# An MLP and an attention moved from a two-block tail into the loop over gathered experts

## What is computed

```python
def peer_ffn(h, w_q, sub_keys, u_tab, v_tab):      # last layer of the first network, per block of 128 rows
    ...                                            # 8 heads; each picks 16 of 16384 experts per row
    act = jax.nn.gelu(jnp.einsum('thkd,td->thk', u_tab[idx], xb)) * wts
    return jnp.einsum('thk,thkd->td', act, v_tab[idx])

def sq_relu_mlp(x, w1, w2):                        # w1 1024 x 4096, w2 4096 x 1024
    return jnp.square(jax.nn.relu(x @ w1)) @ w2

def second_block(x, ...):
    for i in range(DEPTH):                         # DEPTH = 2
        if i % 2 == 0:
            h = mixer_sb_ssm(x, ...)               # stick-breaking attention and a state space scan
        else:
            h = mixer_dsa(x, ...)                  # 16-head attention over keys that an index selects
        x = layer_norm_2(ALPHA * x + h, ln_mix_g[i], ln_mix_b[i])
        x = layer_norm_2(ALPHA * x + sq_relu_mlp(x, mlp_w1[i], mlp_w2[i]), ln_ffn_g[i], ln_ffn_b[i])
    return x
```

## Time and profile before

| | us |
|---|---|
| median of three executions | 3682.71 |
| the profiled execution, device time | 3654.87 |
| its span, first to last instruction | 3653.6 |
| TensorE busy | 2616.1 (72%) |
| VectorE busy | 2061.5 (56%) |
| ScalarE busy | 518.2 (14%) |
| GpSimd busy | 1516.7 (42%) |
| mean granted clock of TensorE, of full speed | 0.821 |
| read from memory | 1152.84 MB |

### The profile page before, as it was taken

How to read it: one execution, slowest core, us unless ns; L and a number is a source line. 1 busy time by engine, 2 the same in 40 slices (tenths; PEclk the granted TensorE clock), 3 DMA queues, 4 the chain that set the end, 5 groups by cost and what they waited for, 6 DMA issues and landing times.

```text
span 3653.6 us, 35023 instructions
## 1 busy us (share of the span) xinstructions
PE 2616.1 (72%) x12888; PEld 1202.7 (33%) x12888; DVE 2061.5 (56%) x5112; ACT 518.2 (14%) x1007; POOL 1516.7 (42%) x1609
## 2 busy tenths in 40 slices
PE   6688777755556865655588585556665889899998
PEld 1233222111112321111154221112312575767765
DVE  0367777656667667866404577666898354231411
ACT  1121011100012111100022110001210122020200
POOL 0035556546666666666500156666566210000000
PEclk8889888788667887767789687776867899999999
DMA  8789999999999999999822599998999786667577
GB/s 308 257 310 363 357 393 379 403 401 389 366 350 364 385 367 354 337 361 366 310 104 81 208 364 391 363 366 333 393 358 347 263 303 223 207 256 253 216 246 263
DMA packets 363672, 1156.36 MB, mean 317 GB/s; under 512 B 33712, under 2 KB 33968, under 8 KB 362476
## 3 DMA queue, kind: packets, MB, share of 16 engines
q0 software_dynamic: 232144, 849.51, 61.4%
q1 hardware_dynamic: 130940, 304.36, 23.2%
q10 hardware_dynamic: 416, 0.23, 0.0%
HBM read 1152.84 MB, written 1.15 MB: 316 GB/s over the span
## 4 chain that ended last, share of the span: by engine, by line
PE 39%; DVE 21%; DMA 20%; POOL 8%; issue 7%; another core or an unknown queue 3%; ACT 2%; SPq 0%; DVEq 0%; ACTq 0%; POOLq 0%
DMA BIG<-in_p_v_dram,IDX 12%; POOL BIG L2363 8%; PE PS L1158 8%; DVE BIG L1959 8%; PE PS L1092 7%; PE PS L1380 6%; PE PS L1362 6%; DMA BIG<-in_p_u_dram,IDX 4%; PE PS L1256 2%; PE PS L1350 2%; DMA WR<-in_w_mod_dram 1%; PE PS L1120 1%; DVE SC L2157 1%; DVE I L1883 1%
## 5 line engine op out<-in xcount | busy, mean ns | idle before, releaser
L1158 PE MATMUL PS<-BIG,DG 64*64 64x512 f32 x6144 | 1057.6, 814 | 674.0 <-DMA BIG<-in_p_v_dram,IDX 500.4
L2363 POOL DMA_INDIRECT BIG<-in_p_u_dram,IDX x768 | 735.1, 957 | 1021.4 <-ACT SCU L1525 242.5
L1959 DVE CUSTOM_DVE_ANT_0 BIG<-BIG,PS 128x1024 f32<-128x1024 f32 x768 | 927.9, 1215 | 312.7 <-DMA BIG<-in_p_u_dram,IDX 272.9
L2363 POOL DMA_INDIRECT BIG<-in_p_v_dram,IDX x768 | 738.6, 962 | 345.7 <-issue 180.4
L1158 PEld LDWEIGHTS PS<-BIG,DG 64*64 64x64 f32 x6144 | 274.4, 168 | 1342.3 <-issue 1220.1
L1092 PE MATMUL PS<-WR,HT 128*128 128x512 f32 x640 | 297.8, 619 | 10.0 <-DMA WR<-in_a_w_in_dram 4.6
L1362 PE MATMUL PS<-HT,WR 128*128 128x128 f32 x2048 | 259.8, 288 | 5.5 <-DVE mv L1807 4.9
L1362 PEld LDWEIGHTS PS<-HT,WR 128*128 128x128 f32 x2048 | 251.0, 203 | 15.5 <-issue 8.9
L1380 PE MATMUL PS<-WR,BIG 128*128 128x512 f32 x512 | 226.2, 597 | 0.0
L1092 PEld LDWEIGHTS PS<-WR,HT 128*128 128x128 f32 x640 | 123.5, 198 | 177.2 <-issue 168.5
L1380 PEld LDWEIGHTS PS<-WR,BIG 128*128 128x128 f32 x512 | 97.1, 192 | 117.4 <-issue 117.1
(11 more groups left out here) (320 smaller groups left out, 2714.0 us busy)
## 6 DMA issues: line engine op xcount, KB each, us to landing
WR<-in_mlp_w_dram SPq DMA_DIRECT2D x128, 1024.0 KB
WR<-in_w_mod_dram SPq DMA_DIRECT2D x48, 1024.0 KB
WR<-in_b_w_in_dram SPq DMA_DIRECT2D x18, 1024.0 KB
WR<-in_a_w_in_dram SPq DMA_DIRECT2D x16, 1024.0 KB
WR<-in_p_w_q_dram SPq DMA_DIRECT2D x16, 1024.0 KB
BIG<-in_dsa_w_dram POOLq DMA_DIRECT2D x16, 1024.0 KB, 7.6
BIG<-in_p_u_dram,IDX POOLq DMA_INDIRECT x768
BIG<-in_p_v_dram,IDX POOLq DMA_INDIRECT x768
```

The lines of the kernel that those rows point to most:

```text
L1158: mm = self.e.matmul(pv[64 * i:64 * i + 64, 2 * r + n, :], dg[p, :], row[p, n * 512:n * 512 + 512], start=h == 0 and j == 0, stop=h == 7 a ...
L1959: self.e.tensor_tensor_reduce(row, row, xp, 1.0, 0.0, ALU.mult, ALU.add, m.ACTV[:, u % 4, j:j + 1]).then_inc(*self.done("dot", l, u, j))
L2363: self.e.indirect_dma_start(row, None, m.A[f"p_{table}"], bass.IndirectOffsetOnAxis(ap=m.IDX[:, u % 4, j:j + 1], axis=0)).then_inc(*m.GR.l ...
```

## The change

The background of block 1's experts is no longer mixer 0 of block 0 alone but a chain (`block_ahead`): mixer 0, stepped with 1 instead of 2 waiting steps, MLP 0 and mixer 1 of block 0. This MLP is cut into parts (`mlp_parts`): part s makes slab s of the up product, squares it, and adds the down product of slab s - 1 into `X` at once, so that `F` (which lies where the gathers go) is not needed. Two yields of a part go to one step of the loop (`"more"`). In the loop a part's PSUM comes from the 2-bank ring (`place` 0), in the tail from the banks of `UP` and `DOWN` (`place` 1). What is left of the chain when the loop ends runs before the barrier.

The tail has then: mixer 0 of block 1 with the first five parts of block 0's MLP 1; block 1's MLP 0 alone; mixer 1 of block 1 with the parts left; block 1's MLP 1 alone. `mlp_first` is gone. MLPs of block b use column b + 2 of `HT` instead of column 2. A new tile `E` holds keys, values and index values of block 0's attention, so that they outlive the next mixer in `H`. The causal masks of mixer 1 go from GpSimd (`affine_select`) to VectorE. In the attention's steps, the later stages of older heads are now written ahead of the new head's product.

```diff
--- before.py
+++ after.py
@@ -235,23 +235,28 @@
+        E = sb("E", [128, 1456])
...
+        self.FS = [Slots([x[:, 512 * i:512 * i + 512].rearrange("p (f t) -> p f t", f=4) for i in range(2)])
+                   for x in (X[:, 2, :], BIG[:, 14336:15360])]
+        self.RS = Slots([X[:, 3, 512 * i:512 * i + 512] for i in range(2)])
@@ -343,9 +348,8 @@
-        mlp = self.mlp(0, 0)
-        self.peer(1, [0, 1], rest, [({0}, self.sb(0, 2))], self.mlp_first(mlp))
-        self.tail(mlp)
+        self.peer(1, [0, 1], rest, [({0}, self.block_ahead())])
+        self.tail()
         self.end()
@@ -644,7 +648,8 @@
-                    next(extra, None)
+                    if next(extra, None) == "more":
+                        next(extra, None)
@@ -652,10 +657,7 @@
-        if close:
-            run(extra)
-        run(ends, iter(close))
-        run(extra)
+        run(ends, extra)
@@ -796,41 +798,85 @@
+    def block_ahead(self):
+        yield from self.sb(0, 1)
+        self.done.note("mixed", 0)
+        self.mlp_begin(0, 0)
+        yield
+        for part in self.mlp_parts(0, 0, 0):
+            yield from part
+        self.dsa_early(0)
+        yield
+        self.mixed(0)
+        yield from self.dsa(0)
+    def tail(self):
 
         self.barrier("tail")
         self.m.side = self.m.WB
-        for i, (early, mixer) in enumerate(((lambda: self.sb_early(1), self.sb(1, 1)),
-                                            (lambda: self.dsa_early(0), self.dsa(0)),
-                                            (lambda: self.dsa_early(1), self.dsa(1)))):
-            early()
-            if i:
-                for _ in zip(range(7), mlp):
-                    pass
-                self.mixed(i - 1)
-            self.beside(mlp, mixer, i)
-            mlp = self.mlp((i + 1) // 2, (i + 1) % 2)
-        run(mlp)
-    def beside(self, mlp, mixer, i):
-        def noted():
-            yield from mixer
-            self.done.note("mixed", i)
-            yield from beats(8)
-        other = noted()
-        for n, _ in enumerate(mlp):
-            for _ in range(2 if n % 3 or not i else 1):
+        self.sb_early(1)
+        self.mlp_begin(1, 0)
+        parts = self.mlp_parts(1, 0, 1)
+        self.beside(self.sb(1, 1), parts, 5)
+        self.done.note("mixed", 1)
+        self.dsa_early(1)
+        self.mlp_begin(0, 1)
+        run(self.mlp(0, 1))
+        self.mixed(1)
+        self.beside(self.dsa(1), parts, 9)
+        self.mlp_begin(1, 1)
+        run(self.mlp(1, 1))
+    def beside(self, mixer, parts, count):
+        def some():
+            for part in parts:
+                yield from part
+                count[0] -= 1
+                if not count[0]:
+                    return
+        count = [count]
+        other = some()
+        for n, _ in enumerate(mixer):
+            if n % 2:
                 next(other, None)
-            if n == (37 if i else 32):
-                run(other)
-                self.mlp_begin((i + 1) // 2, (i + 1) % 2)
+        run(other)
+    def mlp_column(self, l, b):
+        return 2 + b
 
     def mlp_begin(self, l, b):
         tag = ("mlp", l, b)
-        self.flip(tag, 2, self.m.X[:, b, :], self.m.dve.at("normed block", ("dsa_out" if l else "sb_out", b)))
+        self.flip(tag, self.mlp_column(l, b), self.m.X[:, b, :],
+                  self.m.dve.at("normed block", ("dsa_out" if l else "sb_out", b)))
+    def mlp_parts(self, l, b, place):
+        m, tag = self.m, ("mlp", l, b)
+        after = self.flipped(tag, [self.mlp_column(l, b)])
+        def part(s):
+            if s < 8:
+                self.load_slab(("w1", l, b, s), m.A["mlp_w1_2"][l], s * 512)
+                for j in range(4):
+                    self.part_up(l, b, s, j, after, place)
+                    if j % 2:
+                        yield "more"
+                self.part_square(l, b, s, place)
+            if s:
+                for k in (4 * s - 4, 4 * s - 2):
+                    self.load_w2(l, b, k)
+                for n in range(2):
+                    self.part_down(l, b, s - 1, n, place)
+                    yield "more"
+            if s == 8:
+                gain, shift = (*tag, "g"), (*tag, "b")
+                self.load_bc(gain, m.A["ln_ffn_g_2"][l], ())
+                self.load_bc(shift, m.A["ln_ffn_b_2"][l], ())
+                self.norm_block(tag, b, gain, shift)
+                yield
+        return (part(s) for s in range(9))
 
@@ -997,25 +1034,33 @@
-        yield from together(self.select(b), self.dsa_project(b))
+        if b:
+            yield from together(self.index_part(b), self.dsa_project(b))
+        else:
+            yield from self.index_part(b)
+            yield from together(self.select(b), self.dsa_project(b))
         self.dsa_products(b, 0)
         for h in range(16 + 3):
+            if 3 <= h:
+                self.dsa_outs(b, h - 3)
+            if 2 <= h < 18:
+                self.dsa_spread(b, h - 2)
             if h + 1 < 16:
                 self.dsa_products(b, h + 1)
             if h < 16:
                 self.dsa_scores(b, h)
-            if 2 <= h < 18:
-                self.dsa_spread(b, h - 2)
-            if 3 <= h:
-                self.dsa_outs(b, h - 3)
             yield
         yield from self.out_and_norm(("dsa_out", b), b, (m.A["ln_mix_g_2"][1], m.A["ln_mix_b_2"][1]),
                                      lambda k: m.d_out[:, k, :], [m.act.at("dsa out", b, 15)])
 
@@ -1381,6 +1426,42 @@
+    def part_down(self, l, b, s, n, place):
+        m = self.m
+        if place:
+            both = m.DOWN.of(l, b, s) if n else m.DOWN.take(l, b, s)
+            ps = both[:, n, :]
+            self.wait_ge(*m.DOWN.emptied(l, b, s))
+        else:
+            ps = m.PS.take("part down", l, b, s, n)
+            self.wait_ge(*m.PS.emptied("part down", l, b, s, n))
...
@@ -2300,25 +2416,32 @@
     def score_mask(self, b):
-        sc = self.m.d_score[:, 0:128 * b + 128]
-        self.ts(sc, sc, (32.0 ** -0.5) * (8.0 ** -0.5), None, ALU.mult, None, "scores", b)
+        m = self.m
+        sc, last = m.d_score[:, 0:128 * b + 128], m.d_score[:, 128 * b:128 * b + 128]
+        self.ts(sc, sc, (32.0 ** -0.5) * (8.0 ** -0.5), None, ALU.mult, None)
+        self.wait_ge(m.pool.at("strict"), self.done.last())
```

More of the change, by code:

```diff
@@ L599, in others, with peer @@
             yield from work
-    def peer(self, l, order, late, more, close=()):
+    def peer(self, l, order, late, more):
         m, A = self.m, self.m.A
@@ L1713, in square, with part_square @@
         m.UP.free((l, b, n), self.done.last())
+    def part_square(self, l, b, s, place):
+        m = self.m
+        up, relu = (m.UP, m.RM) if place else (m.PS, m.RS)
+        rl = relu.take("part", l, b, s)
+        self.wait_ge(m.pe.at("part up", l, b, s, 3), *relu.emptied("part", l, b, s))
+        self.e.activation(rl, up.of("part", l, b, s), ACT.Relu).then_inc(*self.done("part relu", l, b, s))
+        up.free(("part", l, b, s), self.done.last())
     def dsa_index(self, b):
```

125 lines of the change are left out of this document (82 added, 43 removed).

## The result

| | before | changed |
|---|---|---|
| median | 3681.6 us (3663.0 to 3682.8) | 3716.7 us (3707.2 to 3733.4) |
| ratio | | 1.0112, 95% interval 1.0059 to 1.0165 |
| span of the profiled execution | 3653.6 us | 3707.8 us |

A forecast was written before the change was run, and what follows sets the result against it. Experts' stage bound by gathers, tail by TensorE; moving work between them: scan units to 2763, heads 14 to 16 to 3003, bare attention to 3059, plus tail 578 gives 3637 us against 3653.6 (-0.5%); own range 3645 to 3690, 8-in-10 3615 to 3738.

The forecast's parts named there:

- Heads 9 to 13: Experts' loop units with block 0's mixer 0 at the denser pace: 268 us instead of 261.5, bounds 255 and 280.
- the 95%: VectorE's assumed busy share over heads 9 to 13, turning its 255 us of work into 268 us.
- over 285 us and the forecast falls: Sign for the scan's units: longer than this, VectorE was the limit and one step per step too dense.
- Heads 14 to 16: Last experts' units with the moved MLP and weight loads: 240 us, 127.6 before, transfers and TensorE limits of the same size.
- Rival B: Stretch of the MLP parts: TensorE waits for loads and its clock drops, 3697 us, +1.2%; chance 0.17.
- Rival A: Heads 14 to 16: queues stay full at 404 GB/s, 213 us there, whole 3604 us, -1.4%; chance 0.28.
- Bare attention: Block 0's attention behind the last expert sum, uncovered: 19 steps in 40 us plus output product 16, so 56 us.
- Rival C: Bare attention heads are latency, 4 us a step in block 0, 3.3 in block 1: 3694 us, +1.1%; chance 0.09.
- The tail: Everything behind block 0's attention product: 578 us in all, from 769 before.
- Mixer 0 of block 1: In the tail with five MLP parts: 120 us at VectorE's scan pace plus 30 behind it, 150 us.
- Attention of block 1: In the tail with three ups and four downs: 134 us of TensorE, 141 us with heads at VectorE's pace.
- The 6 us for matmuls at the lower clock: Tail allowance for matmuls run slower behind five waits, raising 572 to 578 us.

The follow-up runs named there:

- e1: Kernel before with block 0's mixer 0 behind the experts at the changed kernel's denser pace: units 9 to 13 300.8 us, ratio 1.0045.
- e7: Changed kernel without the last 8 of 15 spreading steps of block 0's scan: unit 12 12.9 us shorter, median down 13.9 us.
- e10: Changed kernel with heads inside the experts, parts where TensorE waited for norms, and the scan evened between units 12 and 13: ratio 0.9986 to the kernel before.
- e8: Changed kernel without every second down matmul in the eight parts, loads kept: stretch of the parts 147.6 us against 145.7.
- e5: Changed kernel unedited, measured again in another group: ratio 1.0169 to the kernel before, span 3582.0 us.
- e4: Changed kernel with block 0's attention heads taken inside the last two heads' experts: ratio 1.0081 to the kernel before.
- e11: As e10, with four parts beside mixer 0 of block 1 and two beside its attention: ratio 0.9980 to the kernel before.
- e2: Changed kernel with block 0's attention back in the tail, mixer 0 of block 1 bare: ratio 1.0056 to the kernel before.
- e3: Changed kernel with the five parts beside mixer 0 of block 1 begun later and spread: that stage 163.0 us, ratio 1.0128 to the kernel before.
- e9: Kernel before, unedited, traced again on another chip: tail 769.0 us.
- e12: As e11 without the evening of the scan between units 12 and 13: ratio 0.9975 to the kernel before.

## Why the prediction was wrong, step by step

**Heads 9 to 13 (268 us; 299.3).** This step failed, and its 31 us alone are more than the 17 us forecast as gain. VectorE's sum was right (255.6 us, forecast 255), the 95% was not: I took it from the densest window of 55 us and applied it to five units. The same stretch of the earlier trace rows had VectorE at 229.25 of 261.5 us, 88%, and 255 / 0.88 = 290 would have been nearer; the changed kernel has 85%. The prediction named its own test: over 285 us and the forecast falls.

Units 9 and 12 of the kernel before:

```profile
2495.30:2543.20 47.90, 37.12 (x210) 16.57 (x210) 39.41 (x103) 13.03 (x23) 25.79 (x27) 0.75 0.80 283
...
2662.50:2705.10 42.60, 27.25 (x158) 9.18 (x154) 41.02 (x122) 9.15 (x18) 26.08 (x27) 0.74 0.96 368
```

Unit 12 went from 42.6 to 72.9 us, 30 us more, with 26.6 us more of VectorE's work in it. Unit 9 went from 47.9 to 63.8 us, 16 us more for 7.7 us of VectorE's; the other three together are 8 us shorter. e1 shows the pace as the cause, and e7 that unit 12 is VectorE's. The last unit has only 33.5 us of VectorE's work and is held by its transfers (48.8 us, share 1.02). That the uneven load costs the time is not shown: e10 moved work from unit 12 to unit 13, where the transfers are full, and gained nothing. What holds the first unit was not tried.

**Heads 14 to 16 (240 us; 235.3).** The sum was right, and so was the reason, two limits of the same size (e8 and the trace beside it). Inside it two errors cancel, which is luck: the stretch of the parts took 144.9 us where my terms give at most 131: TensorE ran for 134 us without a gap, and ahead of that it had waited 8.1 us for the norm, which I had put at nothing; the two units behind it took 90.4 us of the 109 left. **Rival B** is out: a clock of 0.96 over the parts and 0.3 us of waits for their weights (e5's trace). The Trainium skill ("TensorE: Matmul & The Clock Gate", HAM oscillation) was cited for it. In the changed kernel its case did not arise, since TensorE did not wait. In e8 it did, and its effect is there but small: the 56 up matmuls behind each of the three longest waits (4.04 to 5.96 us) took 8.36 to 9.32 us, where those behind 1.22 us took 6.52, and the granted clock of the stretch was 0.90. **Rival A** had the rate (392 GB/s in the stretch of the parts) but not for long enough: 276 GB/s in the last two units, whose last 18 us have hardly any transfers.

The Trainium skill ("DMA: Bandwidth & Descriptors", Specifications) has about 358 GB/s as a core's share. As a limit for this one core the trace does not agree with it: 392 GB/s over 144.9 us.

**Bare attention (56 us; 64.8).** Steady steps took 1.77 us, under my 2.1, and the product 15.6 where I had assumed 16 (its last piece times four is 14.4 us, not the 13.7 of my text). From the last sum to the product 49 us passed instead of 40. At the start TensorE waited for VectorE and ScalarE (3.6, 3.4 and 1.3 us, at the first products and the spreads between them); VectorE still had the experts' last additions and their norm in its list. **Rival C** in its form (4 us a step) is out. What is true of it is that bare heads cost latency in both blocks, more than my terms held: e4 hides block 0's for 12 us, e11 shows block 1's.

**The tail (578 us; 605.4).** Four terms.
- The start took 12.8 us instead of 18; each MLP alone with the norms and flips on both its sides took 134.5 and 134.2, where my terms give 9.5 + 112 + 10 = 131.5.
- Mixer 0 of block 1: 171.6 instead of 150, the largest miss here. I added 120 us for the scan's pace and 30 behind it, as if parts in TensorE's idle time cost nothing there. The trace shows TensorE full for the first 75 us (74.2 busy, VectorE 35.3), then VectorE with 58.4 of 70.2 us and TensorE at 44.8. The order had shown it: taken at every second place, the five parts are used up by the middle of the mixer. Bare it takes 126.9 (e2), with five parts spread 163.0 (e3).
- Attention of block 1: 152.3 instead of 141. TensorE was busy for 140.6 at a clock of 0.88, 7 more than my 134, and 6.0 us of the rest are one wait behind the last norm of block 0, which stood in VectorE's queue between two heads (L1514 above).
- The 6 us for matmuls at the lower clock are in these numbers and can't be told apart.

**Start (+7.7).** Open. The moved work all lies behind the start of unit 9, and executions of the kernel before differ by 20 us in all within one group (3637.5 to 3657.0). But on each chip with traces of both kinds the kernels built on the changed one came later than those built on the one before: 2495.1, 2502.8 and 2504.3 us (e2 to e4) against 2484.9 (e1), and 2510.9 and 2515.8 (e10, e11) against 2505.6 (e9). With one trace of each, chance and a small cost of the changed kernel (its tiles lie in other places) can't be told apart.

In sum: 31 + 8 + 9 + 27 - 5 us above 3637 is 3707, the measured span. The direction was wrong because two terms that were a sum of work for two engines, heads 9 to 13 and mixer 0 of block 1, were taken with hardly any loss between them: together they are 53 us over.

## What to carry to other kernels

Price background work unit by unit: in each the fullest resource counts, and a density read from the densest window does not hold for the stage. Before moving work out of a stage, ask what it covered there: the MLP saved 93 us and cost 93, since the mixer it left went bare. An order that is a loss can still hold a gain: the places where the tensor engine waits for a norm took independent pieces of its work at little cost, and with these, the heads inside the loop and the parts spread, the same move came out 0.25% ahead (e12).

## What the runs showed of the hardware

On the faster chip the changed kernel's stretch behind the last routing matmul took 3582.0 - 2676.4 = 905.6 us, on the slower one 3707.8 - 2802.3 = 905.5. The whole difference of 126 us lies ahead of that: 118 us ahead of unit 9, and 8 us in units 9 to 13 (291.5, 299.3). That fits the ratio, which is larger on the faster chip (1.0169): by its trace the kernel before is bound by gathers in the last three units, where in the changed one TensorE runs without a gap while the MLP's large loads come at 392 GB/s on both chips. No trace of the kernel before was taken on the faster chip, so this last step is argued, not shown.
